# Scores and outputs of paired half heads and heads, issued by turns on the two halves of TensorE

## The reference, cut to what matters

```python
# first block, differential attention: 8 heads, each of two half heads (c) of 64 features
s = einsum('bhcqd,bhckd->bhcqk', q, k) * 64 ** -0.5
p = softmax(s + bias)                      # causal, slope by head
w = p[:, :, 0] - lam * p[:, :, 1]
o = einsum('bhqk,bhkd->bhqd', w, v)        # then normed by head
# both blocks, memory attention: 4 heads of 128 (twice) or 256 features, not causal
# second block, causal attention of 8 heads ("moba"; one block of keys covers all 256 tokens)
o = softmax(mask(q @ k.T * 64 ** -0.5)) @ v    # 64 features, values 64 wide
# second block, retention: 4 heads, 64 features, values 128 wide
o = ((q @ k.T) * decay) @ v                # equal to the chunkwise form, then normed by head
```

## Time and profile before

| | before |
|---|---|
| median of three executions | 1480.52 us |
| the profiled execution | 1478.86 us |
| its span, first to last instruction | 1477.0 us |
| TensorE matmul busy | 1452.9 us, 98% of the span |
| TensorE weight load busy | 1224.2 us |
| VectorE busy | 828.9 us, 56% |
| ScalarE busy | 687.7 us, 47% |
| granted TensorE clock, mean | 0.995 of full speed |
| share of TensorE in the chain that ended last | 95% |

### The profile page before, as it was taken

How to read it: one execution, slowest core, us unless ns; L and a number is a source line. 1 busy time by engine, 2 the same in 40 slices (tenths; PEclk the granted TensorE clock), 3 DMA queues, 4 the chain that set the end, 5 groups by cost and what they waited for, 6 DMA issues and landing times.

```text
span 1477.0 us, 18731 instructions
## 1 busy us (share of the span) xinstructions
PE 1452.9 (98%) x7412; PEld 1224.2 (83%) x7412; DVE 828.9 (56%) x927; ACT 687.7 (47%) x899; POOL 43.2 (3%) x96
## 2 busy tenths in 40 slices
PE   8999999999999999999999999999999999899997
PEld 6888889988888888888888788888787989788886
DVE  5655565865454555455666464554865565554454
ACT  6545445454444544435445455444544444544442
POOL 1000000000000000000000000000100100000000
PEclk9999999999999999999999999999999999999999
DMA  9755554445555455554444346455433543255551
GB/s 356 260 193 189 181 177 166 171 154 213 178 196 190 152 203 196 189 184 169 171 143 143 114 173 254 174 197 180 176 115 114 189 168 143 100 199 199 181 191 57
DMA packets 38574, 262.14 MB, mean 177 GB/s; under 512 B 4288, under 2 KB 4544, under 8 KB 7648
## 3 DMA queue, kind: packets, MB, share of 16 engines
q1 hardware_dynamic: 37152, 252.85, 48.4%
q0 software_dynamic: 1344, 8.16, 1.4%
HBM read 259.95 MB, written 1.05 MB: 177 GB/s over the span
## 4 chain that ended last, share of the span: by engine, by line
PE 95%; ACT 1%; DVE 1%; SPq 1%; DMA 1%; issue 0%; POOL 0%; POOLq 0%; DVEq 0%; ACTq 0%
PE prod L1001 15%; PE prod L1003 15%; PE prod L1002 15%; PE acc L1001 9%; PE acc L1003 9%; PE acc L1002 9%; PE prod L995 4%; PE prod L996 4%; PE prod L997 4%; PE acc L1168 2%; PE aux L1031 2%; PE acc L1018 1%; DMA raw<-in_weights_dram 1%; PE acc L1187 1%; PE o_bank L1220 1%; ACT acts_h L1319 0%
## 5 line engine op out<-in xcount | busy, mean ns | idle before, releaser
L1489 DVE TENSOR_TENSOR w_lo<-raw,w_hi 128x2048 fp32r<-128x2048 f32 x235 | 538.2, 2291 | 341.3 <-ACT w_hi L1301 341.1
L1301 ACT CAST w_hi<-raw 128x2048 fp32r<-128x2048 f32 x235 | 448.0, 1907 | 293.6 <-PE acc L1003 177.3
L1001 PE MATMUL prod<-w_hi,acts_h 128*128 128x512 f32 x944 | 375.9, 398 | 2.5 <-DVE w_lo L1497 1.7
L1003 PE MATMUL prod<-w_hi,acts_l 128*128 128x512 f32 x944 | 368.8, 391 | 0.0
L1002 PE MATMUL prod<-w_lo,acts_h 128*128 128x512 f32 x944 | 368.4, 390 | 0.0
L1001 PE MATMUL acc<-w_hi,mix_h 128*128 128x512 f32 x600 | 236.7, 395 | 0.3 <-DVE small L1581 0.3
L1003 PE MATMUL acc<-w_hi,mix_l 128*128 128x512 f32 x600 | 233.8, 390 | 0.0
L1002 PE MATMUL acc<-w_lo,mix_h 128*128 128x512 f32 x600 | 233.5, 389 | 0.0
L1001 PEld LDWEIGHTS prod<-w_hi,acts_h 128*128 128x128 f32 x944 | 177.8, 188 | 42.9 <-issue 7.0
L1003 PEld LDWEIGHTS prod<-w_hi,acts_l 128*128 128x128 f32 x944 | 177.5, 188 | 37.7
L1002 PEld LDWEIGHTS prod<-w_lo,acts_h 128*128 128x128 f32 x944 | 177.9, 188 | 35.1 <-issue 0.5
(11 more groups left out here) (255 smaller groups left out, 1220.9 us busy)
## 6 DMA issues: line engine op xcount, KB each, us to landing
raw<-in_weights_dram SPq DMA_DIRECT2D x235, 1024.0 KB, 4.9
raw<-in_weights_dram SPq DMA_DIRECT2D x12, 256.0 KB, 6.6
work<-in_mem_dram POOLq DMA_DIRECT2D x2, 1024.0 KB, 13.4
grow<-in_gain_rows_dram POOLq DMA_DIRECT2D x4, 512.0 KB, 4.4
tabs<-in_tabs_dram POOLq DMA_DIRECT2D x1, 1696.0 KB, 9.4
work<-in_x_t_dram SPq DMA_DIRECT2D x4, 256.0 KB, 6.3
x_res<-in_x_dram SPq DMA_DIRECT2D x1, 1024.0 KB, 8.7
work<-in_mem_t_dram POOLq DMA_DIRECT2D x1, 1024.0 KB, 14.4
```

The lines of the kernel that those rows point to most:

```text
L1001: pe.matmul(out, still_hi, wh, start=first, stop=False, skip_group_check=True)
L1003: return pe.matmul(out, still_lo, wh, start=False, stop=last, skip_group_check=True)
L1301: act.copy(w_hi[:, c % RING], raw[:, c % RAW]).then_inc(hi_done, 1)
L1489: dve.tensor_tensor(w_lo[:, c % RING], raw[:, c % RAW], w_hi[:, c % RING].bitcast(F32), ALU.subtract).then_inc(lo_done, 1)
```

## The change

`ticks` takes groups of units. In the differential section each group is one head with its two half heads, in the moba and retention section two neighbouring heads, which lie on the two halves of the rows of one tile; memory heads are groups of one. A tick's S, F, V and L become lists. Outside draining, the whole group is scored in one tick, and the tick after a group of two has no S (`rest`). The T of each unit comes two ticks after its S at the earliest; for a pair of moba heads, which share an output tile, both V stand in one tick. Retention has no T, its V comes two ticks after its S. Slots of softmax weights (`slot_free`) are now checked when S is planned. On TensorE the order in a tick becomes S, V, T.

In `scores` all waits of the pair come first and the matmuls go by turns: first matmul of one, first of the other, second of one, second of the other. `outputs` does likewise for a pair that makes 64 output rows each. VectorE waits for the scores of both.

```diff
-    def ticks(self, units):
+    def ticks(self, groups):
...
+            showing = to_show[:1]
+            if showing and not showing[0][1]["closes"]:
+                showing = to_show[:2] if len(to_show) > 1 else []
+            if any(unit["need_v"] is None or not unit["free"]() for _, unit in showing):
                 yield "blocked"
                 continue
...
+            if to_turn and (to_turn[0][1]["u"] - 2 < first_u or to_turn[0][1]["u"] - 2 in shown):
+                j, unit = turned = to_turn[0]
+                unit["late"] = self.draining
+                slot_free.add(j)
+                tick["T"] = (unit, j)
+            if rest:
+                rest -= 1
+            elif todo and all(unit["need"] is not None for unit, _ in todo[0]):
+                group = todo[0][:1] if self.draining else todo[0]
+                if all(j - 3 < first or j - 3 in slot_free for j in range(self.j, self.j + len(group))):
...
+                    tick["S"] = to_weigh
+                    rest = len(group) - 1
...
-    ticks = pl.ticks(heads + memory)
+    ticks = pl.ticks([[unit] for unit in heads + memory])
...
-    ticks = pl.ticks(moba + ret)
+    ticks = pl.ticks([heads[n:n + 2] for heads in (moba, ret) for n in range(0, len(heads), 2)])
...
             def scores(it):
...
+                for unit, comp, j in it["S"]:
+                    pe.wait_ge(prod_read, unit["need"])
...
+                for t in range(2):
+                    for unit, comp, j in it["S"]:
+                        r0, r1 = unit["rows"] or (64 * comp, 64 * comp + 64)
...
+                            mm = pe.matmul(bank[:, at:at + width], dests[k][r0:r1, kt, t * P:(t + 1) * P],
+                                           dests[q][r0:r1, qt, S - width:S], start=True, stop=True)
...
+                        if t == 1:
+                            mm.then_inc(score_done, 1)
...
             def outputs(it):
...
+                for n in range(unit["out_tiles"]):
+                    for t in range(2):
+                        for unit, j in it["V"]:
...
+                            if t == 0:
+                                pe.matmul(out, vt[:, 0, c:c + w], src[:, 0:S], start=True, stop=False,
+                                          skip_group_check=True)
+                                continue
+                            mm = pe.matmul(out[:, to], vt[:, 1, c:c + w], src[:, late], start=False, stop=True,
+                                           skip_group_check=True)
...
             def tick(it):
                 if it["S"]:
                     scores(it)
-                if it["T"] and it["T"][0]["table"] != "decay":
-                    turn_weights(it)
                 if it["V"]:
                     outputs(it)
+                if it["T"]:
+                    turn_weights(it)
...
-                    dve.wait_ge(score_done, j + 1)
-                    dve.wait_ge(o_done, unit["u"] - 2)
+                    dve.wait_ge(score_done, unit["scored"][comp])
+                    reader(dve, unit["slot_free"])
```

More of the change, by code:

```diff
@@ L284, in project_tokens @@
             self.to_read(2)
-    def ticks(self, units):
[L292 to L298, removed]
+    def ticks(self, groups):
+        todo = [[(unit, comp) for unit in group for comp in range(unit["comps"])] for group in groups]
+        first, first_u, rest = self.j, self.u, 0
+        slot_free, shown = set(), set()
+        weighed, to_turn, to_show, put_out = [], [], [], []
+        while todo or weighed or to_turn or to_show or put_out:
+            tick = {"S": [], "F": weighed, "T": None, "V": [], "L": put_out, "acc_taken": self.acc_taken,
+                    "banks_read": self.bank_reader[-2:]}
+            showing = to_show[:1]
+            if showing and not showing[0][1]["closes"]:
+                showing = to_show[:2] if len(to_show) > 1 else []
+            if any(unit["need_v"] is None or not unit["free"]() for _, unit in showing):
@@ L299, in ticks @@
                 yield "blocked"
                 continue
[L301 to L327, removed]
+            to_weigh, turned = [], None
+            for j, unit in showing:
                 unit["is_out"] = True
                 unit["late_v"] = self.draining
-                if unit["out"] == "mix" and unit["closes"]:
-                    put_out = unit
@@ new lines, in ticks @@
+            if not any(tick[k] for k in "SFTVL"):
+                yield "blocked"
+                continue
+            for unit in put_out:
+                for n in range(unit["out_tiles"]):
+                    self.mixed += 1
+                    self.tile_at[unit["tile"] + n] = self.mixed
+            put_out = [unit for _, unit in showing if unit["out"] == "mix" and unit["closes"]]
+            del to_show[:len(showing)]
+            if turned:
+                to_turn.pop(0)
+                to_show.append(turned)
@@ L333, in ticks @@
+            for unit, comp, j in weighed:
+                if comp < unit["comps"] - 1:
+                    slot_free.add(j)
+                elif unit["table"] == "decay":
+                    to_show.append((j, unit))
+                else:
+                    to_turn.append((j, unit))
+            weighed = to_weigh
             self.add("tick", **tick)
@@ L470, in make_plan @@
     units = mem_units(4, P, "xq")
-    ticks = pl.ticks(units)
+    ticks = pl.ticks([[unit] for unit in units])
     slot = slots(ticks)
@@ L1145, in scores @@
             def scores(it):
[L1146 to L1170, removed]
@@ L1171, in scores @@
-                mm.then_inc(score_done, 1)
+                for unit, comp, j in it["S"]:
+                    pe.wait_ge(prod_read, unit["need"])
+                    if unit["rope"]:
+                        pe.wait_ge(roped, unit["rope"])
+                    if j in plan.late_steps:
+                        for told in it["banks_read"]:
+                            reader(pe, told)
+                    else:
+                        reader(pe, it["acc_taken"])
+                    for earlier in (j - 2, j - 1) if j in plan.late_steps else (j - 2,):
+                        reader(pe, plan.score_reader.get(earlier))
@@ L1192, in outputs @@
             def outputs(it):
[L1193 to L1208, removed]
+                for unit, j in it["V"]:
+                    pe.wait_ge(prod_read, unit["need_v"])
+                    if unit["table"] == "decay":
+                        pe.wait_ge(decayed, unit["d"])
+                    else:
+                        pe.wait_ge(turned_read, unit["t"])
+                    reader(pe, it["o_free"])
+                    if unit["out_tiles"] == 1 and unit["half"] == 1:
+                        for told in it["banks_read"] if unit["late_v"] else [it["acc_taken"]]:
+                            reader(pe, told)
@@ L1209, in outputs @@
+                unit, j = it["V"][0]
                 if unit["out"] == "norm":
-                    out = bank[:, 0:S]
+                    v, col = unit["v"]
+                    vt, out = tok_dests[v], output_at(unit)[:, 0:S]
+                    src = p_slots[j % 3] if unit["table"] == "decay" else pt_slots[unit["u"] % 2]
                     pe.matmul(out[:, 0:P], src[:, 0:P], vt[:, 0, col:col + P], start=True, stop=True)
                     pe.matmul(out[:, P:S], src[:, P:S], vt[:, 0, col:col + P], start=True, stop=False)
[L1213 to L1222, removed]
@@ L1449, in _ @@
                         ins.then_inc(exp_done, 1)
[L1450 to L1455, removed]
+                    for unit, j in it["V"]:
+                        if unit["out"] == "mix" and unit["closes"]:
+                            act.wait_ge(o_done, unit["u"] + 1)
+                            n = unit["out_tiles"]
+                            act.copy(mix_h[:, unit["tile"]:unit["tile"] + n].rearrange("p a b -> p (a b)"),
+                                     output_at(unit)[:, 0:n * S]).then_inc(o_hi, 1)
                 elif kind == "pool_split":
@@ L1563, in tick @@
             def tick(it):
[L1564 to L1567, removed]
+                for unit, comp, j in it["F"]:
+                    weights(unit, comp, j)
+                for unit in it["L"]:
                     dve.wait_ge(o_hi, unit["o_hi"])
@@ L1820, in number @@
                     late_readers = late_readers[-1:] + [plan.score_reader[j]]
-            if it["T"] and it["T"][0]["table"] != "decay":
+            if it["V"]:
+                it["o_free"] = o_reader[it["V"][0][0]["half"]]
+            for unit, j in it["V"]:
+                n["outs"] += 1
+                assert unit["u"] + 1 == n["outs"]
+                if unit["table"] == "decay":
+                    slot_reader[j % 3] = ("o_done", n["outs"])
+                if unit["out"] == "mix" and unit["closes"]:
+                    n["o_hi"] += 1
+                    unit["o_hi"] = n["o_hi"]
+            if it["T"]:
+                unit, j = it["T"]
                 n["turned"] += 1
```

(15 more changed lines are left out.)

69 lines of the change are left out of this document (55 added, 14 removed).

## The result

| | before | changed |
|---|---|---|
| median | 1480.55 us (4 runs, 1479.03 to 1480.96) | 1461.92 us (4 runs, 1459.07 to 1462.68) |
| ratio to before, 95% interval | | 0.9878 (0.9867 to 0.9890) |
| profiled execution / span | 1478.86 / 1477.0 us | 1459.07 / 1457.3 us |
| TensorE matmul busy | 1452.9 us | 1433.8 us, 98% of the span |
| VectorE / ScalarE busy | 828.9 / 687.7 us | 828.2 / 687.1 us |

A forecast was written before the change was run, and what follows sets the result against it. TensorE, busy 98% of the span, was taken to bound the kernel. Fewer 64-row visits (-5.6), fewer 64-column visits (-1.4), overlap (-5.2) and a wait gone (-0.3) gave -12.5, so 1468.0 us; range 1463.5 to 1475.5.

The forecast's parts named there:

- TensorE's sequence is the time: Whole kernel: TensorE is busy 98% of the span, so a change counts by what it does to TensorE's instruction sequence.
- 0.40 us a visit in the 64-row form: Half-head and 64-feature scores: each visit takes 0.40 us over its passes; 14 fewer visits save 5.6 us.
- 4 fewer output visits: Moba outputs: eight V become four pairs, four fewer visits in 64-column form at 0.34 us, saving 1.4 us.
- By turns on the two halves, 5.2 us: Paired scores and outputs: partial overlap saves 0.22 us in 12 causal pairs and 0.43 in 6 others, 5.2 us.
- The bound of 11.7: Paired scores and outputs: most that overlap could save, 18 x 0.65 us, if both halves ran fully beside each other.
- The cited rules: TensorE, from the skill: changing tiling mode drains, changing tile does not; matmuls start and end strictly in order.
- Waits that go: First output projection's mask wait goes, -0.3 us; at the last norm-head turn 1.2 to 1.6 stays, taken at 0.
- Waits that come: Second half head's mask and exponential: 1.8 us of added work fits 2.9 us of slack; taken at 0.
- The rival of a new wait: Softmax weights: a chunk's cast between mask and exponentials makes T 0.8 us late in 14 pairs; 1479.2 us, chance 0.08.
- Signs: Changed timeline: pair of scores about 0.40 + 1.08 us (0.40 + 0.65 if full overlap); 64-row passes stay 112.
- full overlap: Paired scores and outputs: rival with both halves side by side, loads too; 1461.5 us, chance 0.05.

The follow-up runs named there:

- e3: The kernel before, with all scores of half heads and 64-feature heads contracted over all 128 rows: 1470.4 us, ratio 0.9930.
- e4: The changed kernel, with the second score of each pair contracted over all 128 rows, so forms alternate: 1474.7 us, ratio 0.9965.
- e2: The changed kernel, with both scores of a pair computed on rows 0 to 63: 1471.0 us, ratio 0.9935.
- e6: The changed kernel, with both outputs of a moba pair written into output rows 0 to 63: 1462.7 us (2 runs).
- e1: The changed kernel, with each pair issued one head after the other in scores and outputs: 1459.8 us, ratio 0.9870.
- e8: The changed kernel, with each score matmul of a pair cut into 64-column pieces, issued by turns: 1471.1 us, ratio 0.9944.
- e5: The changed kernel, with pairs issued one head after the other and each score matmul cut into 64-column pieces: 1487.0 us, ratio 1.0049.

## Why the prediction was right and wrong, point by point

- *TensorE's sequence is the time.* Right: 19.0 of 19.7 us lie in the two sections, and the visits account for them. In the differential section 8 visits fewer, each 0.40 and a hidden side of 0.65, and two shorter waits make 8 x 1.05 + 0.34 + 0.32 = 9.1 (measured 9.3). In the moba section 6 x 1.05 for scores and 4 x 0.99 for outputs, less 0.4 for a wait that grew, make 9.8 (measured 9.7).
- *0.40 us a visit in the 64-row form.* Right, and shown by removal (e3: 1.05 to 0.65, 10 us) and by adding changes (e4: 0.20 each). The 14 fewer score visits and 4 fewer output visits were counted rightly; 7.0 us stands.
- *By turns on the two halves, 5.2 us.* This is the step that failed: the term of the sum for the overlap. It was worth 18 x 0.65 = 11.7 us, the prediction's own bound, as e2 and e6 confirm in the visits (1.70 against 1.05, 1.92 against 1.28). Two assumptions under the 5.2 were false. First, passes were stepped as if each were an instruction that starts in program order, A A B B. But the other half's first pass starts 6 ns after the first pass of this half, ahead of its second, and even past one waiting matmul (e1). Second, the 0.11 us between loads was read on the full array, where there is one stream of them, and carried over to two halves, which load side by side (e8).
- *The chances.* The row nearest to the unknown was not near: no row of before had neighbours on different halves. The bound of 11.7 was rightly priced, but given a chance of 0.05 on the strength of that carry-over, and the range left it out. With the 11.7 the sum is -19.0 and the median 1461.5, and 1461.9 was measured.
- *The cited rules.* That changing the tiling mode drains TensorE and changing the tile does not ("TensorEngine Tiling (Array Packing)", Key Properties, in the Trainium skill) agrees with the runs on both counts: 0.20 us for each of the four changes in e4, and nothing for a change of half in the changed kernel. The rule of strictly ordered starts ("TensorE: Matmul & The Clock Gate", Part 3, in the Trainium skill) does not hold as it stands: in e1 and e5 a matmul of the other half starts ahead of one that waits, and only beyond that one does the order hold. What the same part says of neighbours on different row groups, that they start some 4 ns apart, is near the 6 to 8 ns seen here.
- *Waits that go.* The wait of the first output projection on the mask, 0.34, is gone. The wait behind the last head turn is 1.34 instead of 1.66 us, in the 1.2 to 1.6 that was worked out. Timeline of PE, changed kernel:

```profile
812.34 0.60 PE L1326 MATMUL aux<-tabs,sq 128*128 128x128 f32 x4
812.77 1.03 PE L1197 MATMUL prod<-mem_k,obuf 128*128 128x256 f32 x4
...
816.01 0.63 PE L1217 MATMUL aux<-tabs,four 128*128 128x128 f32 x4 [1.34 <-DVE mix_l L1820]
```

- *Waits that come.* None on the softmax weights. Timeline of DVE, changed kernel, the last mask of the first pair and the end of its weights:

```profile
718.11 0.42 DVE L1617 CUSTOM_DVE_ANT_0 masked<-tabs,acc 128x256 f32<-128x256 f32 x1
...
720.46 0.75 DVE L1594 SCALAR_TENSOR_TENSOR sq<-sq,small,four 128x128 f32<-128x128 f32 x2
```

  The weights are done at 721.21, and the transposes of that head start at 723.17, 2 us later; 2.9 - 1.8 = 1.1 had been worked out. The rival of a new wait did not occur. One wait grew: the first moba scores wait 1.3 us on the values' projection, where it was 0.8. VectorE ends that projection's copy as early as before (at 1058.94 in the changed kernel and 1067.76 before, 7.29 us after the k rotation's mark in both), but the first score starts 0.47 us behind it and not 0.06. In the changed kernel's trace four semaphore instructions of TensorE's queue, 0.11 us apart (1058.98 to 1059.31), stand in between, where the kernel before has none. The new code puts all waits of a pair ahead of its first matmul, so these are the likely cause; no run takes them away alone, and at the other visits, where TensorE has no idle time before the pair, they cost nothing that shows.
- *Signs.* The 112 passes of 64 rows are all there, and the visit of a pair is its 0.40 + 0.65 for full overlap: the pair costs what one of them costs.

## What to carry to other kernels

Two equal fp32 matmuls on different halves of the rows or of the weight columns cost what one costs, and no extra change of form, so pair them. With two matmuls a side the order does not matter; with six a side, issue them by turns. A lone visit in a half form inside a stream of full ones costs 0.40 us, so gather such visits. The lone one would take less in the full form, if one operand holds zeros in the rows that are not its own; no run here tried that with right values. When a term has no near row, the range must reach its full bound.

## What the runs showed of the hardware

- A change between the full form and that of 64 rows costs 0.20 us each way, about half of it a weight load that is not hidden, also in the middle of a visit (e4: 2.09 us with four changes). For 64 weight columns both ways together cost 0.34.
- Matmuls on the two halves start 6 to 8 ns apart when issued by turns and 13 to 15 when one head's two stand ahead, with loads side by side; two column halves do so even into one bank.
- A matmul for the other half overtakes one waiting matmul of this half (e1), but waited while more than one stood waiting (e5: 0.95 us, until the fifth of six had started).
- A pass on half the array is as fast as on all of it: some 0.11 us for 128 columns and 0.22 for 256, and so with both halves at work.
